# A mixture-of-experts stage: three gated sums of the last pair but one placed inside the last pair's up projection, and the order of the sums that follow

## What is computed

```python
# 16 experts; each token gets gates for its top 2 experts
hid = silu(einsum('nd,edf->nef', xf, w_gate)) * einsum('nd,edf->nef', xf, w_up)     # f = 256
y = einsum('nef,efd->nd', hid * gates[..., None], w_down)                           # d = 1024
# layer: y_tokens = y_tokens + y; then the next layer's rmsnorm (or the final one)
```

## Time and profile before

| | |
|---|---|
| time, median of 3 runs | 610.3 us (608.62 to 613.45) |
| profiled execution, time | 606.24 us |
| profiled execution, span of the core | 604.3 us |
| mean granted TensorE clock | 0.989 of full speed |
| PE busy | 571.8 us, 95% of the span |
| DVE busy | 246.1 us, 41% |
| ACT busy | 154.1 us, 26% |
| from HBM / to HBM | 198.76 MB / 43.74 MB, 401 GB/s over the span |

### The profile page before, as it was taken

How to read it: one execution, slowest core, us unless ns; L and a number is a source line. 1 busy time by engine, 2 the same in 40 slices (tenths; PEclk the granted TensorE clock), 3 DMA queues, 4 the chain that set the end, 5 groups by cost and what they waited for, 6 DMA issues and landing times. The chain is left out here.

```text
span 604.3 us, 8599 instructions
## 1 busy us (share of the span) xinstructions
PE 571.8 (95%) x3470; PEld 332.1 (55%) x3470; DVE 246.1 (41%) x598; ACT 154.1 (26%) x329; POOL 85.7 (14%) x113
## 2 busy tenths in 40 slices
PE   6999999999969999999999999999999999999893
PEld 5677877545733434336977555667646733444330
DVE  6999673122832112145551614260112841221126
ACT  6132295121301101024235203254012301101022
POOL 5991600000021210000100001000000031110000
PEclk9999999999989999999999999999999999999998
DMA  8996998498899999999899998999699789999962
GB/s 342 399 333 70 243 394 307 153 417 355 336 421 385 419 421 422 397 323 375 313 421 328 407 394 312 320 360 408 241 422 419 291 312 415 422 420 422 419 180 92
DMA packets 39930, 208.94 MB, mean 346 GB/s; under 512 B 12819, under 2 KB 14547, under 8 KB 23920
## 3 DMA queue, kind: packets, MB, share of 16 engines
q1 hardware_dynamic: 30416, 169.92, 72.9%
q0 software_dynamic: 7872, 34.53, 16.0%
q10 hardware_dynamic: 1600, 3.90, 1.7%
HBM read 198.76 MB, written 43.74 MB: 401 GB/s over the span
## 5 line engine op out<-in xcount | busy, mean ns | idle before, releaser
L1378 PE MATMUL bank<-arena 128*64 128x512 f32 x272 | 80.2, 597 | 5.9 <-DVE arena L1680 3.1
L1378 PE MATMUL bank<-ring,arena 128*64 128x512 f32 x240 | 72.9, 597 | 3.6 <-DVE arena L1680 3.6
L2124 PE MATMUL bank<-arena,ring 128*128 128x320 f32 x256 | 71.6, 434 | 0.0
L2124 PEld LDWEIGHTS bank<-arena,ring 128*128 128x128 f32 x256 | 48.0, 190 | 21.4 <-issue 1.6
L1304 PE MATMUL bank<-ring,arena 128*128 128x512 f32 x104 | 45.4, 594 | 1.0 <-PEq L447 0.6
L1791 DVE TENSOR_TENSOR arena<-arena,bank 128x256 f32<-128x256 f32 x16 | 6.7, 422 | 94.4 <-ACT arena L1585 94.4
L1378 PEld LDWEIGHTS bank<-arena 128*64 128x64 f32 x272 | 25.4, 137 | 35.9 <-issue 35.7
L1378 PEld LDWEIGHTS bank<-ring,arena 128*64 128x64 f32 x240 | 23.3, 137 | 33.8 <-issue 33.6
L558 PE MATMUL bank<-xnT,ring 128*128 128x320 f32 x144 | 41.2, 447 | 0.5 <-DVE xnT L876 0.5
L1409 PE MATMUL bank<-arena 128*64 128x512 f32 x136 | 39.8, 593 | 0.0
L1409 PE MATMUL bank<-ring,arena 128*64 128x512 f32 x120 | 36.2, 592 | 0.0
(11 more groups left out here) (447 smaller groups left out, 874.4 us busy)
## 6 DMA issues: line engine op xcount, KB each, us to landing
arena<-in_w_moe SPq DMA_DIRECT2D x51, 1024.0 KB, 19.4
ring<-in_w_moe SPq DMA_DIRECT2D x45, 1024.0 KB, 15.1
arena<-in_stream_b SPq DMA_DIRECT2D x4, 2560.0 KB, 14.4
out_o_d_old<-in_cache_d_g POOLq DMA_DIRECT2D x1, 8448.0 KB, 29.5
arena<-in_stream_a SPq DMA_DIRECT2D x4, 2048.0 KB, 10.8
out_o_d_old<-in_cache_d_g POOLq DMA_DIRECT2D x1, 7680.0 KB, 42.4
out_o_d_old<-in_cache_d_g SPq DMA_DIRECT2D x1, 4608.0 KB, 37.8
ring<-in_w_out_even SPq DMA_DIRECT2D x2, 2048.0 KB, 11.7
```

Source lines behind the costliest of these rows:

```text
L1378: last = nc.tensor.matmul(c.bank[2 + j % 2][half, :], xgT[:, j % 2, q, half], w[i][:, q, :], start=(q == 0), stop=(q == KC - 1))
L2124: last = nc.tensor.matmul(bank(name)[:, 0:TOK], w[:, k, i * P:(i + 1) * P], xnT[:, k, :], start=(k == 0), stop=(k == KC - 1))
```

## The change

In the last pair's up projection, ahead of step 4, TensorE now makes `sum_samples(0)` and `sum_rows(0, 1, 1)`, with the three waits that stood before ahead of the first sum. These two calls are three matmuls, the "three sums". They used to stand behind `down(7)`. Behind `down(7)` the sums of the first tile, `sum_rows(1, 0, 0)` and `sum_rows(1, 0, 1)`, now come at once, each behind its wait on `yo`, and `sum_rows(0, 1, 0)` follows them. For the other pairs the two calls of `up` issue what the one call did. The same holds in both layers, as `moe_block` runs for each. No instruction is added or taken away, and no other engine's list changes.

```diff
             for j in range(PAIR_N):
-                up(j, 1, KC)
-                if j + 1 < PAIR_N:
-                    turn(j + 1)
+                up(j, 1, KC // 2)
                 if j == LAST:
                     pe.wait_ge(gate_sb, 2)
                     pe.wait_ge(yo_a, LAST)
                     pe.wait_ge(yo_b, LAST)
+                    sum_samples(0)
+                    sum_rows(0, 1, 1)
+                up(j, KC // 2, KC)
+                if j + 1 < PAIR_N:
+                    turn(j + 1)
+                if j == LAST:
                     sum_rows(0, 0, 0)
                 turn_hidden(j)
                 if j == LAST:
...
-            sum_samples(0)
-            sum_rows(0, 1, 0)
             pe.wait_ge(yo_a, PAIR_N)
             sum_rows(1, 0, 0)
             pe.wait_ge(yo_b, PAIR_N)
             sum_rows(1, 0, 1)
-            sum_rows(0, 1, 1)
+            sum_rows(0, 1, 0)
             sum_rows(1, 1, 0)
             sum_rows(1, 1, 1)
```

## The result

| | before | changed |
|---|---|---|
| median, 20 runs each | 607.98 us (604.17 to 613.51) | 610.24 us (606.68 to 614.22) |
| ratio to before, 95% interval | | 1.0058, 1.0038 to 1.0079 |
| profiled execution, time / span | 606.24 / 604.3 us | 609.52 / 607.6 us |
| mean granted clock in it | 0.989 | 0.987 |
| PE busy | 571.8 us | 574.4 us |

The changed kernel is slower, by less than one per cent. The medians are 2.3 us apart, and the ratio is 3.5 us of 608 (2.3 to 4.8 us). The two differ in part because the ratio is taken over undisturbed runs alone, without the two of before that lie more than 1.5% above its fastest (613.45 and 613.51 us), while the medians are over all twenty. The 610.3 us of before that the prediction started from was the median of three of these twenty runs.

What follows compares the result with a forecast made beforehand. TensorE, busy 571.8 of 604.3 us, was taken as the path. Per layer 2.07 + 1.05 - 1.92 = 1.20 us later, over two layers 2.4 us: 610.3 + 2.4 = 612.7 us, range 609.5 to 615.4 us.

Steps and rivals of the forecast that it cites:

- Step 1 and 2: Per layer, 1.92 us of sums removed behind down(7), and 2.07 us added in the last pair's up projection.
- Step 3: Behind down(7), TensorE waits bare for ScalarE's copy: 0.95 us, with a slow second instruction 1.05 us per layer.
- Step 4: Behind tile 0's sums, sum_rows(0, 1, 0) replaces sum_rows(0, 1, 1): no cost, and tile 0 first brings nothing.
- Does it reach the end: Both layers hand their 1.20 us on to the end, 2.4 us together; the weights' wait in layer 1 stays 2.8 us.
- One layer only: Rival, chance 0.20: layer 1's weights' wait shrinks, or late rows bind VectorE there; only one layer pays, 611.5 us.
- Filled wait: Rival, chance 0.07: at step 4 of the last pair, the sums fill a wait for weights' second halves; faster, 608.6 us.
- More lost than one copy: Rival, chance 0.11: step 4 waits for pair 6, or width changes inside accumulation cost more; 0.7 us more per layer, 614.1 us.

Runs made afterwards that it cites:

- the samples' sums alone: Against the changed kernel, sum_rows(0, 1, 1) moved back behind down(7), only sum_samples(0) left in the up projection: layer 0 0.00 us, layer 1 +0.14 us against before.
- the wide sum alone: Against the changed kernel, sum_samples(0) moved back behind down(7), only sum_rows(0, 1, 1) left in the up projection: layer 0 +0.35 us, layer 1 +0.53 us against before.
- the second trace of the changed kernel: The changed kernel run again with no edit, beside before on the same chip: median 608.29 against 605.44 us, ratio 1.0033.
- the kernel with one sum back: Against the changed kernel, sum_rows(0, 1, 0) moved ahead of the wait on yo_a behind down(7): median 608.08 against before's 605.44 us, ratio 1.0011.

## Why the prediction was right

The forecast was 612.7 us, within 1% and slower, by 2.4 us over before; measured were 610.24 us and 2.3 us over before's median of the same twenty runs. Its absolute value leaned on a median of three runs that was 2.3 us above that of twenty, and this is the main part of its miss. That the medians give the forecast difference to 0.1 us is luck: the ratios give 3.5 us in this series and 2.0 us in the second. What bears the forecast out is the 2.22 us of the traces, and that each part of the sum was found where it was said to be.

**Step 1 and 2, what is taken away and added: right.** The added piece was forecast at 2.07 us. Step 1 to the first sum behind step 7 takes 583.95 - 575.75 = 8.20 us after and 579.67 - 573.53 = 6.14 us before: 2.06 us. That a satisfied wait and an interrupted sum cost nothing was an assumption, and the samples' sums alone have shown it. The price of the two changes of width (0.35 us with the wide sum alone) was read off correctly.

**Step 3, the bare wait: right in kind, 0.08 us too dear.** The one mis-sized term is the release: 0.14 us by the earlier trace rows, and 590.52 - 590.46 = 0.06 us by the copy's row in the new trace. With it 1.20 becomes 1.12 us, which both traces of the changed kernel show in layer 0, with 1.10 us in layer 1. What is shown of the cause: with the wait bare and nothing moved up the loss is as large, though that kernel too has two changes of width more; with a sum in front of the wait 1.34 of 2.22 us are back; and what is left in layer 0 then, 0.36 us, is what the wide sum costs alone, 0.35 us. So of the 1.12 us about 0.35 us are changes of width and 0.76 us the wait.

**Step 4, tile 0 first brings nothing: right**, and shown more sharply than claimed, since even 0.97 us earlier brought nothing.

**Does it reach the end: mostly.** In layer 1 it does, with VectorE's two waits for TensorE where they were. From layer 0 the 1.12 us were handed on through the mixer: SyncE issues 485.71 - 290.50 = 195.21 us behind the next mixer's first matmul before, and 486.41 - 291.14 = 195.27 us in the changed kernel:

```profile
486.41 4.25 SPq L134 DMA_DIRECT2D ring<-in_w_moe  x4
```

The prediction held that the wait for weights would stay at 2.8 us. It was 2.58 and 2.37 us. From the next mixer's first matmul to the end of that wait it takes 278.72 us before and 278.59 and 278.33 us in the changed kernel, and in the two kernels that came to that matmul 4.4 and 4.6 us later than before, mostly for clock falls further up, 277.52 and 277.65 us with waits of only 1.59 and 1.50 us. So a TensorE that is 4.5 us late seems, by these two traces, to get back about 1.1 us. For 1.12 us of lateness nothing of the kind is shown: the second trace of the changed kernel issued at 485.71 us and came to the mixer at 290.49 us, both as before, and its weights still landed 0.40 us earlier, so that this much comes and goes by itself. Whether a part of the stream runs on a clock of its own is open; it was not tried.

**The rivals.** One layer only: out, both layers pay. Filled wait: out, no wait at step 4 in any trace. More lost than one copy: out, 1.12 us in a layer and not 1.9. The clock fall was not among the rivals. It accounts for 1.70 of the 3.3 us between the two profiled spans, and whoever reads the change's price off those spans gets half again too much.

## What to carry to other kernels

Work that an engine does between the last product and the wait for its copy is the cover of that copy. Count it in us against the copy, from the producer's last slot to the release (here 0.86 us), before moving any of it ahead of the producer; one sum of 0.96 us is enough, as the kernel with one sum back shows. Keep matmuls of another width out of a run of narrow ones (one wide sum cost 0.35 us here). Pulling forward what another engine needs brings nothing while that engine isn't the one that ends last, and pushing it back costs only what exceeds that engine's idle time (0.14 us here).

## What the runs showed of the hardware that was not expected

The granted clock fell to one half at places that differ from run to run: around step 0 of the last pair twice in seven traces, and in the kernel with one sum back for 10.2 us from 97 us on, where two other traces show a fall of 3.4 and 6.8 us and seven show none. On the page a fall of 3.4 us is an 8 among forty slices, and it is easier seen in a run's mean clock: in the twenty runs of the changed kernel the four at 0.989 took 606.68 to 609.17 us and the five at 0.981 or less took 610.64 to 614.22 us. A change of half a per cent is smaller than this spread, and pieces of the trace cut at the same instructions told it to 0.02 us (1.12 and 1.12, 1.10 and 1.10 us in two executions).

A wait for ScalarE is over sooner than the earlier trace rows had it: 0.06 us after the copy's end, against 0.14 us there.
